# State space outputs of the S5 heads: partial products combined on VectorE, two matmul terms instead of four

## The reference, cut to what matters

```
bu_re, bu_im = B_bar u                       # per group, 64 complex states, 16 channels
x_t = a * x_(t-1) + bu_t                     # complex, a = |a| e^(i theta)
y   = C_re x_re - C_im x_im                  # this is where the change is
y   = gelu(y + d * u);  y = y * sigmoid(y W + b)
```

## Time and profile before

| | |
|---|---|
| median of three runs | 2171.57 us (2171.08 to 2173.16) |
| the profiled execution's own time | 2175.82 us |
| its span, first to last instruction | 2174.0 us |
| mean granted clock of TensorE, share of full speed | 0.997 |
| PE busy | 2140.0 us, 98% |
| DVE busy | 1467.9 us, 68% |
| ACT busy | 1028.3 us, 47% |
| POOL busy | 632.0 us, 29% |

### The profile page before, as it was taken

One profiled execution on the slowest core, in us unless ns is written; L12 is line 12 of the kernel. 1 busy time (PEld: TensorE's weight loads), 2 busy tenths in 40 slices (PEclk: granted clock), 3 DMA queues, 4 the chain that ended last, 5 costly groups with the idle time before them and its releaser, 6 DMA issues.

```text
span 2174.0 us, 47257 instructions
## 1 busy us (share of the span) xinstructions
PE 2140.0 (98%) x18496; PEld 2120.8 (98%) x18496; DVE 1467.9 (68%) x1808; ACT 1028.3 (47%) x1338; POOL 632.0 (29%) x628
## 2 busy tenths in 40 slices
PE   8999999999999999999999999999999999999997
PEld 8999999999999999999999999999999999999997
DVE  6798895677666556666666667777665555666665
ACT  5555554444444444444444455445444444444443
POOL 5644430234343003434211111233434003343311
PEclk9999999999999999999999999999999999999999
DMA  6444453555454665555556444555554565555553
GB/s 260 172 163 161 160 188 142 193 178 200 187 198 153 210 211 194 196 190 196 169 189 228 144 143 143 189 185 198 194 191 170 189 208 206 192 194 192 167 196 118
DMA packets 67154, 399.91 MB, mean 184 GB/s; under 512 B 9776, under 2 KB 11696, under 8 KB 31600
## 3 DMA queue, kind: packets, MB, share of 16 engines
q1 hardware_dynamic: 60192, 391.15, 50.5%
q10 hardware_dynamic: 5712, 6.21, 0.9%
q0 software_dynamic: 1152, 1.18, 0.2%
HBM read 395.23 MB, written 2.10 MB: 183 GB/s over the span
## 4 chain that ended last, share of the span: by engine, by line
PE 88%; DVE 6%; issue 2%; ACT 1%; DVEq 1%; DMA 0%; POOLq 0%; POOL 0%; ACTq 0%
PE PS L1557 28%; PE PS L1558 28%; PE PS L1561 28%; DVE lo L768 3%; ACT hi L374 1%; DVEq L983 1%; DVE S L1010 0%; DVE S L1003 0%; PE PS L1920 0%; PE PS L1919 0%; PE PS L1933 0%; PE PS L1679 0%; PE PS L1906 0%; PE PS L1903 0%; PE PS L1619 0%
## 5 line engine op out<-in xcount | busy, mean ns | idle before, releaser
L768 DVE TENSOR_TENSOR lo<-raw,hi 128x1024 fp32r<-128x1024 f32 (+2 forms) x826 | 949.3, 1168 | 499.5 <-ACT hi L374 494.3
L374 ACT ACTIVATE hi<-raw 128x1024 fp32r<-128x1024 f32 (+2 forms) x826 | 786.7, 970 | 742.3 <-PE PS L1561 706.7
L1557 PE MATMUL PS<-XS,hi 128*128 128x256 f32 x3600 | 848.2, 278 | 8.3 <-ACT hi L374 8.3
L1558 PE MATMUL PS<-XS,hi 128*128 128x256 f32 x3600 | 843.5, 277 | 0.0
L1557 PEld LDWEIGHTS PS<-XS,hi 128*128 128x128 f32 x3600 | 677.5, 188 | 11.6 <-issue 11.2
L1558 PEld LDWEIGHTS PS<-XS,hi 128*128 128x128 f32 x3600 | 677.6, 188 | 0.4
L1561 PE MATMUL PS<-XS,lo 128*128 128x256 f32 x3600 | 483.7, 277 | 0.0
L1561 PEld LDWEIGHTS PS<-XS,lo 128*128 128x128 f32 x3600 | 443.9, 188 | 0.0
L1557 PE MATMUL PS<-YF,hi 128*128 128x256 f32 x1408 | 331.8, 276 | 0.0
L1558 PE MATMUL PS<-YF,hi 128*128 128x256 f32 x1408 | 331.7, 276 | 0.0
L1506 POOL TENSOR_TENSOR ctmp<-apad,cws 128x512 f32<-128x512 f32 x88 | 131.9, 1519 | 525.7 <-DVE apad L817 525.7
(11 more groups left out here) (272 smaller groups left out, 2272.9 us busy)
## 6 DMA issues: line engine op xcount, KB each, us to landing
raw<-in_ffn_up SPq DMA_DIRECT2D x176, 1024.0 KB, 4.8
raw<-in_ffn_dn SPq DMA_DIRECT2D x128, 704.0 KB, 4.1
raw<-in_w_in SPq DMA_DIRECT2D x51, 1024.0 KB, 4.9
raw<-in_w_oe SPq DMA_DIRECT2D x16, 1024.0 KB, 4.8
raw<-in_w_oo SPq DMA_DIRECT2D x16, 1024.0 KB, 4.9
raw<-in_mla_dn SPq DMA_DIRECT2D x9, 1024.0 KB, 5.3
raw<-in_w_ukv SPq DMA_DIRECT2D x8, 1024.0 KB, 5.1
raw<-in_w_uq SPq DMA_DIRECT2D x8, 768.0 KB, 4.3
```

The lines of the kernel that those rows point to most:

```text
L374: act.activation(hi[:, p % SLOTS, 0:n], raw[:, u % SLOTS, off:off + n], ACT.Copy).then_inc(hi_ready, 1)
L768: V.tensor_tensor(lo[:, p % SLOTS, 0:n], raw[:, u % SLOTS, off:off + n], f(hi[:, p % SLOTS, 0:n]), ALU.subtract).then_inc(lo_ready, 1)
L1557: mm(PS[:, bank, 0:T], wh, x[:, 0:T], start=first, stop=False)
L1558: mm(PS[:, bank, 0:T], wh, x[:, T:2 * T], start=False, stop=False)
```

## The change

`scan` now lets both multiplications write temporaries (`sT2` and `sB`), drains, and combines them: the real part is a difference, the imaginary part a sum, each of 128 x 512. The result goes to `Z0` for k = 0 and to `sT1` for k = 1. The semaphore `z_ready` is raised by the last of them. `c_x` takes the two parts with two sets of weights. `Z0` is half as large; it lies at the start of a region that other buffers reuse later, so no other buffer moves. POOL's two negations stay as they are.

```diff
-        Z0 = sb("Z0", [P, 2, 2, 2, T], fp32, early)
+        Z0 = sb("Z0", [P, 2, 2, T], fp32, early)
...
                     dve.drain()
                     eb = E[:, k]
-                    za, zb = (Z0[:, 0], Z0[:, 1]) if k == 0 else (sT2, sB)
-                    V.tensor_tensor(za, sT1, eb[:, 0:1].broadcast_to([P, 2, 2, T]), ALU.mult)
-                    V.tensor_tensor(zb, sT1, eb[:, 1:2].broadcast_to([P, 2, 2, T]), ALU.mult).then_inc(z_ready, 1)
+                    zc = Z0 if k == 0 else sT1
+                    V.tensor_tensor(sT2, sT1, eb[:, 0:1].broadcast_to([P, 2, 2, T]), ALU.mult)
+                    V.tensor_tensor(sB, sT1, eb[:, 1:2].broadcast_to([P, 2, 2, T]), ALU.mult)
+                    dve.drain()
+                    V.tensor_tensor(zc[:, 0], sT2[:, 0], sB[:, 1], ALU.subtract)
+                    V.tensor_tensor(zc[:, 1], sT2[:, 1], sB[:, 0], ALU.add).then_inc(z_ready, 1)
...
-                    for i, (c, part, ri) in enumerate(((0, 0, 0), (2, 1, 1), (1, 1, 0), (1, 0, 1))):
+                    for i in range(2):
                         for q in range(4):
-                            z = (Z0[:, part] if q < 2 else (sT2, sB)[part])[:, ri, q % 2, :]
-                            ins = mm(PS[32 * q:32 * q + 32, 6, 0:T], Cst[:, q, c, :], z, start=i == 0, stop=i == 3)
+                            z = (Z0 if q < 2 else sT1)[:, i, q % 2, :]
+                            ins = mm(PS[32 * q:32 * q + 32, 6, 0:T], Cst[:, q, i, :], z, start=i == 0, stop=i == 1)
```

## The result

The changed kernel took 2179.01 us in the median of 7 runs (2177.65 to 2183.37), the kernel before 2172.97 us in 7 runs (2171.08 to 2177.76). The ratio is 1.0034, 95% interval [1.0024, 1.0043]: slower, by 6.0 us between the medians. The forecast was +4.2 us on top of 2171.57, 2175.8 us with a range to 2178.6, and "within 0.2%" as the likeliest. Direction of the working, place of the cost and its size up to `Pm` were right; the time lies 0.4 us above the range.

The account below looks back on a forecast made before the run. In heads 1 to 4 DVE paces some 32 us, PE some 22 us. DVE's 7.64 us cost less PE's 3.44 us saving gave +4.20 on 2171.57, so 2175.8 us; range 2172.4 to 2178.6 us.

Parts of the forecast that it names:

- within 0.2%: Whole kernel: +0.19% forecast, just inside what a measurement tells from none; "same" given chance 0.55.
- PE's saving: c_x in heads 2 to 5: 16 fewer matmul instructions save 0.86 us each, 3.44 us in all.
- DVE's cost at `scan(0)`: Heads 1 to 4: drain and two instructions 1.38 us, extra turn with POOL 0.53; 1.91 per head, 7.64 in all.
- rival 1: No extra turn with POOL: DVE pays only 1.38 us per head, +2.1, 2173.7 us; chance 0.25.
- Rival 3: DVE work hidden after all, only the c_x saving counts: 2168.1 us; chance 0.04.
- rival 4: Matmul saving in c_x absent, two terms cost as long as four: +7.6, 2179.2 us; chance 0.05.
- `scan(1)` ... cost nothing: Added 1.4 to 2.4 us at scan(1) covered by 4.8 us of idle DVE before Q piece 3, less 0.86.
- rival 2: Cover behind scan(1) used up, c_x saving lost in heads 2 to 4: +6.8, 2178.4 us; chance 0.11.
- PE's wait before the retention output stays about 1.06 us: Before Pm in heads 1 to 4: everything behind V piece 2 shifts alike, so none of the DVE cost is hidden.
- +4.20: Whole kernel: net change in us, 7.64 of DVE cost less 3.44 of PE saving.
- It lay 4.25 us above the median of the runs, which I take to stay: Profiled execution of 2175.82 us against the median 2171.57; the same offset assumed after the change.

Follow-up runs that it names:

- PE part alone: Kernel before with c_x cut to two of its four terms, DVE untouched: ratio 0.9988, -2.4 us.
- DVE part alone: Kernel before with the drain and two 128x512 combinations added behind each multiplication pair, into an unread buffer, c_x at four terms: +9.3 us, ratio 1.0041.
- PE kept busy: 14 idle matmuls behind b_u(2) added to the changed kernel (ratio 1.0019 against before) and to the DVE part alone (ratio 1.0045, 2180.87 us).

## Why the prediction was right and where it failed

- **PE's saving, 0.86 us per head:** 0.68 to 0.87 measured (PE part alone), x16 in 1.00 us.
- **DVE's cost at `scan(0)`, 1.38 + 0.53 us:** 1.90 in A, in each of four heads. The 0.53 is POOL's, shown by cutting its sums: both are paid, 0.53 us each, and rival 1, which left this out, is refuted. The Trainium skill (SBUF — State Buffer, "SBUF: two separate sides") has the shared ports held for a whole instruction while the other engine is blocked. The trace agrees: POOL's two sums take 1.12 and 1.70 us instead of 0.75, and DVE's two splits 3.42 instead of 2.36. Rival 3 (hidden work) is refuted by A, rival 4 (no saving) by B.
- **"`scan(1)` ... cost nothing":** right. DVE idled 0.35 us before the reciprocal and 1.07 before Q piece 3, so rival 2 did not come.
- **"PE's wait before the retention output stays about 1.06 us":** this failed, and with it "+4.20". The step counted the wait before V piece 2 as time of PE alone and took PE's speed behind it as given. A wait of 1.9 to 2.7 us there is followed, in two or three heads of four, by a fall to half clock that takes up to 1.7 us of matmul work. The wait at `Pm` absorbs most of it: nothing remains in head 2 of the changed kernel, 0.37 to 0.55 us in its head 1 and in heads 1, 3 and 4 of the DVE part alone; where less waiting is left it is about 1 us, and 1.7 us behind `Pm`. The kernels with PE kept busy show the cause to be the wait: DVE's work is the same there, and no fall is left. I had no rival for the clock, and the trace of the kernel before held a case of it that I did not look at, since it lies in the odd layer: a wait of 1.25 us before the 1-column matmuls at 1231.99 (L1851), and behind it, in stretches of 2 us,

```profile
1232.00:1234.00 2.00, 2.00 (x17) 2.00 (x18) 1.28 (x2) 1.36 (x2) 0.00 (x0) 1.00 0.00 0
1234.00:1236.00 2.00, 2.00 (x15) 2.00 (x15) 0.44 (x2) 0.27 (x1) 0.00 (x0) 0.76 0.36 57
1236.00:1238.00 2.00, 2.00 (x11) 2.00 (x11) 0.74 (x6) 2.00 (x5) 0.00 (x0) 0.50 0.84 332
```

  Some three microseconds at half clock again. One look at the granted clock over the whole span, in short stretches, would have given a price, though not in which heads it is due.
- **"It lay 4.25 us above the median of the runs, which I take to stay":** this failed too. The profile of after was itself the median of its 7 runs. And the median of before is 1.4 us higher in 7 runs (2172.97) than in the three (2171.57). From 2172.97 the same working gives 2177.2 us, and the measured 2179.01 would lie inside a range laid about it in the same way. That the time lies 0.4 us above the range is thus partly the luck of three runs, and not the clock alone.

The account from 2171.57 to 2179.01, 7.4 us: 1.4 the start value; 4.2 the steps worked out; 0.5 more outside the span (2.2 to 2.4 us on average in the changed kernel, 1.8 before); 1.3 is over. The mean spans of the changed kernel and of the one with PE kept busy differ by 1.3 as well (2177.1 and 2175.8, same chip), but that difference is uncertain by more than a microsecond. In the profiles the two falls cost 0.4 to 0.55 us together. The mean clock gives two or three falls a run, by an estimate from the runs: 0.9968 - 0.9947 = 0.0021 of 2177 us is 4.6 us, at 1.7 each. So about half a microsecond to one is the clock, and the rest is not told from the scatter. The sum of the two parts tried alone, 9.3 - 2.4 = 6.9, agrees with the measured 6.0 within their scatter.

What stays open is when a wait lets the clock fall. In the changed kernel run again the same wait of 1.92 us did it in head 2 and not in head 3.

## What to carry to other kernels

Trading matmuls for vector instructions is paid by the place of the vector work, not by its amount: the same two combinations cost 1.9 us per head ahead of `Pm` and nothing 20 us later. Before placing VectorE work, look for the engine that paces that stretch, for idle time further on, and for what GpSimd runs beside it. And a new wait of TensorE costs more than its length when the clock falls behind it, unless a second wait further on absorbs it.

## What the runs showed of the hardware that I had not expected

**The pace of TensorE at full clock has two values.** Before and after, the out projection, with the granted clock at 1.00 and the same instructions:

```profile
380.00:390.00 10.00, 10.00 (x87) 10.00 (x86) 6.51 (x7) 4.65 (x5) 2.26 (x2) 1.00 0.62 229
```

```profile
380.00:390.00 10.00, 10.00 (x91) 10.00 (x90) 7.80 (x9) 4.65 (x5) 2.46 (x2) 1.00 0.62 216
```

87 matmuls in 10 us against 91, and 0.118 against 0.113 us between two starts. In these two profiles the changed kernel is 3.42 us behind at ACT's L374 (363.37 and 366.79) and only 0.01 behind at its L650 (1228.31 and 1228.32), so it gained 3.4 us where nothing was changed. It then lost 2.1 us, again in unchanged code, until L677 (1352.82 and 1354.94), at a granted clock of 1.00 from 1246 us on; why is open. So two profiles of whole kernels can't be subtracted to find a change of this size; the local times can. I take the pace for the main part of the scatter of 2171 to 2178 us in the runs of one kernel, but did not test it.

**Time outside the span.** It is 1.8 us in every run of the kernel before. In the kernels with the shorter `c_x` it is 1.8 in some runs and 2.1 to 3.0 in others, mean 2.2 to 2.6. With the 14 extra matmuls it is 1.8 again. The cause is open.
